# Norms by tiles with two units' products between the last transposes, a quarter row in a bank of its own, and the bridge's sums first

## What is computed

```
h = rms_norm(x, norm_mix_g)                     # norm 0
aq, ak, av, hq, hf, hi, hg, ga, gh = split_combined(h @ w_in)
merged = sigmoid(ga) * (y_attn @ w_attn_proj) + sigmoid(gh) * (y_hgrn @ w_hgrn_proj)
x = x + merged @ w_out
x = x + peer_layer(rms_norm(x, norm_ffn_g), w_peer_q, keys, u, v)   # norm 1
x = rms_norm(x, norm_final_g)                   # the bridge
hn = rms_norm(x, norm_mix_g_2)                  # norm 3
...                                             # second mixer, cross attention (norms 4, 2)
h = h + cross_attention(...)                    # ends with w_xo
hn = rms_norm(h, norm_ffn_g_2)                  # norm 5
h = h + conv_glu(hn, w_up, ..., w_down)
return rms_norm(h, final_g)
```

## Time and profile before

| | us |
|---|---|
| Median of 3 runs | 1447.51 (1447.35 to 1455.02) |
| Profiled execution, its own time | 1447.28 |
| Span of its trace | 1445.5 |
| PE busy in it | 1425.1 |
| Mean granted TensorE clock | 0.998 of full |

### The profile page before, as it was taken

How to read it: one execution, slowest core, us unless ns; L and a number is a source line. 1 busy time by engine, 2 the same in 40 slices (tenths; PEclk the granted TensorE clock), 3 DMA queues, 4 the chain that set the end, 5 groups by cost and what they waited for, 6 DMA issues and landing times.

```text
span 1445.5 us, 25160 instructions
## 1 busy us (share of the span) xinstructions
PE 1425.1 (99%) x10271; PEld 1290.1 (89%) x10271; DVE 966.7 (67%) x1746; ACT 734.4 (51%) x1055; POOL 209.6 (14%) x120
## 2 busy tenths in 40 slices
PE   8999999999999999999999999999999999999998
PEld 7989979999999999998777778888899888899986
DVE  5565674693944777778888876655577864677754
ACT  5673654545454444444444445544567754555543
POOL 5000000488883000000000000000014100000000
PEclk9999999999999999999999999999999999999999
DMA  6433446455555545555555566555443453455553
GB/s 237 145 131 102 162 161 210 140 179 186 180 186 178 172 162 172 165 163 173 175 164 172 168 223 240 186 184 185 160 152 122 152 180 108 158 178 187 187 184 111
DMA packets 66931, 245.07 MB, mean 170 GB/s; under 512 B 7424, under 2 KB 7552, under 8 KB 66560
## 3 DMA queue, kind: packets, MB, share of 16 engines
q1 hardware_dynamic: 66816, 243.45, 50.5%
HBM read 242.37 MB, written 1.05 MB: 168 GB/s over the span
## 4 chain that ended last, share of the span: by engine, by line
PE 93%; ACT 3%; DVE 2%; issue 1%; POOL 1%; DMA 0%; SPq 0%; DVEq 0%; POOLq 0%; ACTq 0%
PE bank L427 92%; ACT A L1038 1%; ACT whi L1038 1%; PE bank L436 1%; DVE wlo L1548 1%; ACT L1038 1%; DVE A L1548 0%; DVE A L1544 0%; DMA raw<-in_w_in_t 0%; POOL wlo L2347 0%; POOL small L2353 0%; DVE xres L1551 0%; DVE xres L1548 0%; ACT hTh L1038 0%; DVE hTl L1551 0%
## 5 line engine op out<-in xcount | busy, mean ns | idle before, releaser
L1548 DVE TENSOR_TENSOR wlo<-raw,whi 128x1024 fp32r<-128x1024 f32 x374 | 457.9, 1225 | 334.0 <-ACT whi L1038 333.5
L1038 ACT ACTIVATE whi<-raw 128x1024 fp32r<-128x1024 f32 x448 | 472.9, 1057 | 403.9 <-PE bank L427 402.5
L427 PE MATMUL bank<-hTh,whi 128*128 128x256 f32 x1944 | 555.2, 286 | 2.3 <-DVE wlo L1548 1.0
L427 PE MATMUL bank<-hTh,wlo 128*128 128x256 f32 x1944 | 548.8, 282 | 0.0
L427 PE MATMUL bank<-hTl,whi 128*128 128x256 f32 x1944 | 547.2, 281 | 0.0
L427 PEld LDWEIGHTS bank<-hTh,whi 128*128 128x128 f32 x1944 | 366.4, 188 | 6.9 <-DVE hTl L1551 2.5
L427 PEld LDWEIGHTS bank<-hTl,whi 128*128 128x128 f32 x1944 | 367.0, 189 | 0.3 <-issue 0.2
L427 PEld LDWEIGHTS bank<-hTh,wlo 128*128 128x128 f32 x1944 | 364.9, 188 | 0.0
L427 PE MATMUL bank<-whi,hTh 128*128 128x512 f32 (+2 forms) x552 | 218.3, 396 | 0.2
L2347 POOL TENSOR_TENSOR wlo<-raw,whi 128x1024 fp32r<-128x1024 f32 x74 | 177.3, 2398 | 274.9 <-ACT whi L1038 271.0
L427 PE MATMUL bank<-wlo,hTh 128*128 128x512 f32 (+2 forms) x552 | 215.0, 390 | 0.0
(11 more groups left out here) (171 smaller groups left out, 1373.4 us busy)
## 6 DMA issues: line engine op xcount, KB each, us to landing
raw<-in_u SPq DMA_DIRECT2D x128, 512.0 KB, 3.3
raw<-in_v SPq DMA_DIRECT2D x128, 512.0 KB, 3.3
raw<-in_w_up SPq DMA_DIRECT2D x44, 512.0 KB, 3.3
raw<-in_w_down SPq DMA_DIRECT2D x22, 512.0 KB, 3.3
raw<-in_w_in_t SPq DMA_DIRECT2D x18, 512.0 KB, 4.2
raw<-in_w_in_g SPq DMA_DIRECT2D x16, 512.0 KB, 3.3
raw<-in_w_out SPq DMA_DIRECT2D x16, 512.0 KB, 3.8
raw<-in_w_pq SPq DMA_DIRECT2D x16, 512.0 KB, 3.5
```

What stands on the lines that cost most here:

```text
L427: return e.matmul(o, l, r, start=st, stop=sp_, skip_group_check=True)
L1038: return e.activation(o, i, func, **kw)
L1548: return e.tensor_tensor(o, a, b, op)
```

## The change

1. **Norms tile by tile** (norms 0, 1 and 5). `norm_head` takes the place of `norm_pe` and of the first two units of `lin_T`. It transposes all of block 0 and four tiles of block 1, waits for the first two units' low parts, spins twice, and then, for each of the 8 tiles, waits for that tile of `hTl`, transposes one more tile of block 1 (in the first four rounds) and makes this tile's products of both units, 6 matmuls. ACT and DVE write `hTh` and `hTl` by single tiles (`norm_hi_tiles`, `norm_lo_tiles`). In norms 1 and 5 the spins ahead of block 1 go from 2 to 1 and those ahead of the products from 4 to 2; norm 0 keeps its 1 and 2.
2. **Block 0 scaled by ACT** (norms 1 and 5): `scaled0` after ACT's squares, with a semaphore of its own.
3. **The last quarter row in a bank of its own** (w_out, w_xo, w_down): the last half of block 1 is finished in two quarters, the second of them into the first 256 columns of the bank that block 0's first half has left. DVE adds the half row as it stands (`r_part`), then the last quarter alone, and sums the squares of that quarter itself.
4. **The bridge**: ACT makes `whi` of w_xk+2 before the squares of the bridge and of w_xk+3 after them; DVE's two sums of norm 3 come one after the other ahead of the scaling.

Which engine makes which unit's low part is not changed.

```diff
+            def norm_head(j, src, u0, spins):
+                for b in range(TB):
+                    if spins[b]:
+                        spin(spins[b], 7)
+                    for k in range(8 if b == 0 else 4):
+                        if b == 0 and k < 4:
+                            use(k)
+                        norm_tile(j, src, b, k)
+                bk = 4 + pair[0] % 3
+                use(bk)
+                wa, wb = (two(unit(u0 + i), KD) for i in range(2))
+                spin(spins[2], 7)
+                for k in range(KD):
+                    e.wait_ge(s["n_lo"], 8 * j + k + 1)
+                    if k < 4:
+                        norm_tile(j, src, 1, k + 4)
+                    h = [z[:, k, :] for z in hTv]
+                    ins = three(banks[bk][:, 0:256], [z[:, k, :] for z in wa], h, k == 0, k == KD - 1)
+                    if k == KD - 1:
+                        ins.then_inc(s["w"], 1)
+                    ins = three(banks[bk][:, 256:512], [z[:, k, :] for z in wb], h, False, k == KD - 1)
+                ins.then_inc(s["w"], 1)
...
-            norm_pe(1, scr, spins=(4, 2))
-            lin_T(BASE["w_pq"], 16, hTv, KD, normed(1, 4))
+            norm_head(1, scr, BASE["w_pq"], (4, 1, 2))
+            lin_T(BASE["w_pq"] + 2, 14, hTv, KD)
...
+            def scaled0(r, dst):
+                e.wait_ge(s["n_rstd"], 2 * r + 1)
+                for c in range(4):
+                    act(dst[:, c * 256:c * 256 + 256], xres[:, c * 256:c * 256 + 256], ACT.Copy, scale=small[:, 2:3]
+                        ).then_inc(s["n_scaled0"], 1)
...
-            residual_squares(0, scr)
+            part_squares(0, scr)
+            scaled0(1, scr)
             hi(BASE["w_pq"] + 1)
-            for k2 in range(4):
-                norm_hi(1, "g_ffn", hTv, k2)
+            norm_hi_tiles(1, "g_ffn")
...
             side.lists[0].append(bridge())
+            hi(BASE["w_xk"] + 2)
             side.step()
-            lin_T(BASE["w_xk"], 6, copy_to(kT2))
+            side.step()
+            hi(BASE["w_xk"] + 3)
+            e.wait_ge(s["w"], BASE["w_xk"] + 2)
+            copy_to(kT2)(0, t3(banks[4 + pair[0] % 3][:, :], 2))
+            pair[0] += 1
+            side.step()
+            lin_T(BASE["w_xk"] + 2, 4, copy_to(kT2, 2))
...
+            def part_add_and_sum(stage, b0, last, r, scratch):
+                add(stage, b0, last, 0, 0)
+                add(stage, b0, last, 0, 1)
+                add(stage, b0, last, 1, 0)
+                rms_sum(r, 0)
+                at = {1: 0, 6: 3, 7: 4}[r]
+                z = xres[:, D + 512:2 * D]
+                e.wait_ge(s["acc2"], ACC2[stage])
+                tt(z, banks[b0 + 3][:, :], z, ALU.add).then_inc(s["r_part"], 1)
+                z = xres[:, D + 768:2 * D]
+                e.wait_ge(s["w"], last)
+                e.wait_ge(s["r_part"], PARTS[at])
+                tt(z, banks[b0][:, 0:256], z, ALU.add).then_inc(s["r_add"], 1)
+                e.wait_ge(s["r_add"], 4 * at + 4)
+                own(stt(scratch[:, D + 768:2 * D], z, 1.0 / D, z, ALU.mult, ALU.mult, accum_out=small[:, 8:9]))
+                again()
+                st = small[:, 4:8]
+                e.wait_ge(s["n_sq"], 4 * r + 4)
+                own(ts(small[:, 9:10], st[:, 0:1], st[:, 1:2], EPS, ALU.add, ALU.add))
+                again()
+                tt(st[:, 3:4], small[:, 8:9], small[:, 9:10], ALU.add).then_inc(s["n_sum"], 1)
...
                 final_scale(3, gfin, 1)
                 rms_sum(4, 0)
+                rms_sum(4, 1)
                 scaled(4, xres, scr3, 0)
-                rms_sum(4, 1)
                 yield
...
-            add_and_sum("w_down", 0, NU, 7)
+            part_add_and_sum("w_down", 0, NU, 7, xs)
             e.wait_ge(s_gf2, 16)
             final_scale(7, gfin2, 0)
-            rms_sum(7, 1)
             final_scale(7, gfin2, 1)
...
             rstd(1)
-            e.wait_ge(s["n_scaled"], 16)
+            e.wait_ge(s["n_scaled"], 12)
             lo(BASE["w_pq"] + 1)
```

More of the change, by code:

```diff
@@ L139 @@
 ACC1 = {name: i + 1 for i, name in enumerate(("w_out", "v", "w2_out", "w_xo", "w_down"))}
+ACC2 = {name: i + 1 for i, name in enumerate(("w_out", "w_xo", "w_down"))}
+PARTS = {0: 1, 3: 2, 4: 3}
+SCALED = (0, 8, 12, 20, 28, 36)
+SCALED0 = {1: 0, 5: 4}
 B_TAPS = (2, 0, 0, 3, 6, 7, 7, 6)
@@ L462, in norm_pe, with norm_tile @@
                     free[bks[k2]] = (s["n_lo"], 8 * j + 2 * k2 + 2)
[L464 to L470, removed]
+            def norm_tile(j, src, b, k):
+                if k % 2 == 0:
+                    if b == 0 and j in SCALED0:
+                        e.wait_ge(s["n_scaled0"], SCALED0[j] + k // 2 + 1)
+                    else:
+                        e.wait_ge(s["n_scaled"], SCALED[j] + (4 * b if j not in SCALED0 else 0) + k // 2 + 1)
+                o = (k // 4 * 2 + b) * P
+                ins = tr(banks[k % 4][:, o:o + P], src[:, b * D + k * P:b * D + (k + 1) * P])
+                if b:
+                    ins.then_inc(s["n_tr"], 1)
@@ new lines, in norm_head @@
+            def norm_head(j, src, u0, spins):
[20 more added lines that the diff above has]
+                ins.then_inc(s["w"], 1)
+                for k in range(4):
+                    free[k] = (s["n_lo"], 8 * j + 4 + k + 1)
+                by, n_ev = PAIR_FREED[pair[0]]
+                free[bk] = (s[by], n_ev)
+                pair[0] += 1
@@ L497, in lin_T, with lin_A @@
                     side.step(steps[(i + 1) % len(steps)])
-            def lin_A(u0, src, K, N, bks, ready, pair=True):
+            def lin_A(u0, src, K, N, bks, ready, pair=True, split=None):
                 per, nh = UNIT // N, N // 512
@@ L878, in pe_program @@
             e.wait_ge(s_keep, 16)
-            norm_pe(0, scr, spins=(0, 1))
-            lin_T(BASE["w_in_t"], 4, hTv, KD, normed(0, 2))
+            norm_head(0, scr, BASE["w_in_t"], (0, 1, 2))
+            lin_T(BASE["w_in_t"] + 2, 2, hTv, KD)
             e.wait_ge(s_con1, 16)
@@ L1023, in head_ready @@
                 e.wait_ge(s["cr_dve"], 6 * (h // 2) + 5 + h % 2)
[L1025 to L1030, removed]
+            lin_A(BASE["w_xo"], oT2, KD, D, (4, 5, 6, 7), head_ready, split=3)
+            norm_head(5, xs, BASE["w_up"], (4, 1, 2))
+            lin_T(BASE["w_up"] + 2, 42, hTv, KD)
+            lin_A(BASE["w_down"], aF, 22, D, (0, 1, 2, 3), lambda k: e.wait_ge(s["ff_lo"], k + 1), split=4)
         def act_program(e):
@@ L1365, in act_program @@
             hi(0)
-            norm_hi(0, "g_mix", hTv, 0)
             hi(1)
-            for k2 in range(1, 4):
-                norm_hi(0, "g_mix", hTv, k2)
+            norm_hi_tiles(0, "g_mix")
             e.wait_ge(s["lb_dve"], 1)
@@ L2183, in dve_program @@
             e.wait_ge(s_keep, 16)
-            for k2 in range(4):
-                norm_lo(0, "g_mix", hTv, k2)
+            norm_lo_tiles(0, "g_mix")
             l0, l1 = C1("lb", 0, 4), C1("lb", 4, 8)
@@ L2234, in dve_program @@
             lin_A(BASE["w_out"], 8, hold=True)
-            residual_norm("w_out", 0, BASE["w_out"] + 8, 1, scr)
-            for k2 in range(4):
-                norm_lo(1, "g_ffn", hTv, k2)
+            part_norm("w_out", 0, BASE["w_out"] + 8, 1, scr)
+            norm_lo_tiles(1, "g_ffn")
             lin_T(BASE["w_pq"], 16)
```

78 lines of the change are left out of this document (60 added, 18 removed).

## The result

The changed kernel takes 1458.03 us (median of 17 runs, 1456.11 to 1465.68) where the kernel before takes 1448.49 (17 runs beside them, 1447.08 to 1455.02). The ratio is 1.0069, 95% interval 1.0056 to 1.0083: slower by 0.7%, outside the range on record. The profiled execution took 1465.68 us, with a span of 1463.9, 18.4 us more than the span of before, so it holds more than a typical run does. What follows takes it apart.

The account below looks back on a forecast made before the run. PE is busy for 99% of the span, so only its waits or empty spins can give time. 2.8 + 1.1 + 1.1 - 3.2 + 1.5 = +3.3 us on 1447.28 gives 1450.6; range 1447.3 to 1453.9.

Parts of the forecast that it names:

- I count one fall, at norm 0: +1.5: Clock term: of PE's pauses at norms 0, 1 and 5, only norm 0's brings half clock, costing +1.5 us.
- 1.5 to 2 us each: Cost of one clock fall, from 3 to 4 us at half clock, each us costing half a us.
- The rival that counts all three: Rival: the clock falls at the pauses of norms 0, 1 and 5; +6.6 us, 1453.9; chance 0.10.
- if the clock fell at other norms: Sign against the forecast: half clock at norms other than norm 0, the only one counted.
- The waits: PE waits longer for POOL's low part of the second unit: +2.8 us at norm 0, +1.1 each at norms 1 and 5.
- The late unit 2: Norm 0: DVE's low part of unit 2 is ready only at 20.7, so PE waits 0.8 us more.
- -3.2 with -2.4 as the other end: Bridge: w_xk+4 starts at 1050.2 instead of 1053.42, -3.2 us; -2.4 if block 1's scaling stays slow beside POOL.
- The tail: End of the program: DVE's final scaling of block 1 starts at 1441.65, as now at 1441.62; no gain.
- The two gains that the change has here, an earlier sum and finer tiles, both end in front of POOL: Norm 1: both gains stop at the wait for POOL's low part, so the sum there is +1.1 us.
- the change does what it says: Rival: norms 1 and 5 gain 1.0 us each, norm 0 even at best, bridge -3.2; 1442.1; chance 0.08.
- slower rival: Rival: half clock holds through the stretches behind the three norms; 1456.6 at 5 us each; chance 0.05.

Follow-up runs that it names:

- e1: The changed kernel with spins put into PE's pause ahead of the wait for the two low parts at norms 0, 1 and 5; 1451.63 us.
- e9: e4 with the wait for POOL's low part of the second unit put back ahead of the first tile; 1454.69 us.
- e7: e4 with the quarter row undone; 1445.62 us.
- e8: e4 with the wait for POOL's low part of the second unit put back ahead of the first tile at norm 0 alone; 1447.29 us.
- e6: The changed kernel without the quarter row, ACT still scaling block 0; 1460.60 us.
- e4: The changed kernel with only the first unit's products between the last transposes; the second unit's follow as a block and alone wait for POOL; 1443.97 us.
- e3: The kernel before with the change's orders of ACT and DVE at the bridge alone; 1446.00 us.
- e2: The changed kernel with the low parts of units 1, w_pq+1 and w_up+1 made by DVE instead of POOL; 1451.52 us.
- e5: The kernel before without its spins at norms 1 and 5; 1448.92 us beside 1448.64.

## Why the prediction was wrong

**The step that failed: "I count one fall, at norm 0: +1.5".** In the profiled execution the clock fell at all three pauses. The term was +1.5 us and measures 4.8 in the profile: 1.8 at norm 0 and 1.5 each at norms 1 and 5 (the changed kernel's steps less e1's). The size of one fall, "1.5 to 2 us each", was right (its "3 to 4 us" at half clock came from no row; each stretch at a norm lasted 3.41); the count was wrong. I had put norms 1 and 5 aside because their pause was shorter, although the only two rows on it were one fall after 2 us of rest at the end and none after the 1.4 us at the bridge. A pause of 2.3 us lies above both. The rival that counts all three had 0.10 and should have been the forecast. The prediction's own last sign, "if the clock fell at other norms", is what came.

The Trainium skill, TensorE: Matmul & The Clock Gate, Part 1, says that the throttled clock is the default and that activity releases it. By that rule the prediction counted all three pauses, +4.8 us, and the trace agrees: 4.8. The same 2.54 us pause at norm 1 without a fall, in e9's trace, shows that it is not so in every execution.

**A second clock term was absent.** The rival with three falls gave 1453.9, and the median is 4.1 us above it. Runs of the changed kernel have a middle mean clock of 0.993 against 0.998, so some 14 us more at half clock, more than three falls' 10.2. One such place is near 1130 us, behind small matmuls; e7's and e8's traces show it too. That the change makes it likelier was not shown.

**The waits were right.** Norm 0: 2.8 forecast, 3.0 (e1). Norms 1 and 5: 1.1 forecast each, 1.3 each. The reasons were right as well: POOL's start is set by block 1's scaling, PE's pause at norm 0 is 3.88 us for 3.9 forecast, and unit 2's low part there is the next thing late. The late unit 2 was forecast with 0.8 us and measures 0.78 in e1.

**The bridge was right in kind, 0.5 us too good.** Forecast -3.2 with -2.4 as the other end; -2.7 in nine traces. The step that slipped is the path between block 0's and block 1's tiles. The prediction had PE's transposes and spins as the last to end. In the chain of work it is DVE's: block 0's scaling, the low part of w_xk+4, then block 1's scaling. They take 1.34, 1.47 and 1.57 us where such operations took 1.15, 1.22 and 1.15 undisturbed, and all three run beside POOL, the last in part. The rule on the shared interface (the Trainium skill, GPSIMD Engine Reference, Specifications) gave -2.4, and the trace lies between the two: POOL's moved part took 2.50 us for 2.37, its power 0.99 beside DVE where undisturbed ones take 0.55.

**The tail was right, the quarter row undervalued.** The tail gives nothing. "The two gains that the change has here, an earlier sum and finer tiles, both end in front of POOL" was half right: the earlier sum also starts POOL sooner, by 0.7 us against the same kernel without the quarter row (e6), which the +1.1 had counted as 0.4. With POOL out of the way it gives 0.8 us a norm (e4 against e7).

**The rival "the change does what it says" was nearly a recipe.** It asked for -1.0 at norms 1 and 5, nothing at norm 0 and -3.2 at the bridge, 1442.1. With POOL's low part out of the first product's way, that is nearly what came: e4 has -0.9, -0.9, +0.2 and -2.7, a span of 4.2 us less than before.

**The chances.** The text put 7.2 us as what a measurement tells; the loss is 9.5. Its slower rival "decides from +7.2 us on, so 11 us at half clock in all, 3.6 at each", and I gave it 0.05 as if the half clock had to last through whole stages. The three falls alone are 3.41 each, a hair under that; three waits 0.2 us longer each, a bridge 0.5 us poorer and one more stretch of half clock carry it over. The range ended at three falls and held nothing for half clock elsewhere.

## What to carry to other kernels

When products of two units are interleaved, the first product waits for the later of the two operands: look at who makes the second, and what used to cover it. Count each new pause of PE twice, once as a wait and once as the half clock behind it. Where the trace has a fall after a pause of that order, expect a fall at every such pause, though single executions can be spared. A change made of parts can hide a gain: here one line, the place of one wait, separates -4.6 us (e4) from +6.1 (e9).

## What the runs showed of the hardware

Every stretch at half clock between the start and the end of a program lasted 3.41, 6.83, 13.65 or 20.48 us, and one of 3.41 us amid dense products cost 1.3 to 1.5 us, one of 20.48 us 9.3, so 0.38 to 0.45 us for each us at half clock. Single kernels' times come in clusters (before: 1447.2, 1448.5, 1450.1, 1454.8, 1457.8), which fits such stretches.

PE need not be idle ahead of a fall. The stretch near 140 us and that near 1130 come behind small matmuls. PE in the timeline of the changed kernel:

```profile
136.34 3.06 PE L431 MATMUL bank<-A 32*128 32x128 f32 x24
139.23 0.37 PE L431 MATMUL bank<-hTh,whi 128*128 128x256 f32 x1
...
139.71 0.42 PE L431 MATMUL bank<-hTh,whi 128*128 128x256 f32 x1
...
1128.08 1.13 PE L431 MATMUL bank<-A 4*128 4x256 f32 x4
1129.14 0.39 PE L431 MATMUL bank<-hTh,whi 128*128 128x256 f32 x1
...
1129.69 0.42 PE L431 MATMUL bank<-hTh,whi 128*128 128x256 f32 x1
```

The distance from product to product goes from 0.12 to 0.21 us within half a microsecond of the small ones' end. It happened near 140 us in the profiles of the changed kernel, e1, e3, e6 and e7 and not in those of before, e2, e4, e5, e8 and e9, with the same code there. Why it lasts 20.48 us in two of them, 13.65 in two and 3.41 in one was not found.
